# A delta-net inversion with its two 64-blocks overlaid, and 16 row products moved from VectorE to GpSimd and ScalarE

## What is computed

```python
decay = jnp.exp(jnp.where(incl, Gcum[..., :, None] - Gcum[..., None, :], -jnp.inf))
kb = kc * bc[..., None]
A = jnp.where(strict, jnp.einsum('bhnid,bhnjd->bhnij', kb, kc) * decay, 0.0)
t_inv = lax.linalg.triangular_solve(A + eye, jnp.broadcast_to(eye, A.shape), left_side=True, lower=True, unit_diagonal=True)
W = t_inv @ (kb * jnp.exp(Gcum)[..., None])
U = t_inv @ (vc * bc[..., None])
...
v_new = U_n - W_n @ S
o = qd_n @ S + attn_n @ v_new
S = S * gt_n + k_tail_n.T @ v_new
```

## Time and profile before

| | us |
|---|---|
| median of 3 runs | 1768.65 (1767.53 to 1769.34) |
| the profiled execution, its time | 1769.91 |
| its span in the profile | 1768.1 |
| mean granted TensorE clock | 0.992 |
| TensorE busy | 1712.0 (97%) |
| VectorE busy | 1299.4 (73%) |
| ScalarE busy | 1075.2 (61%) |
| GpSimd busy | 161.9 (9%) |

### The profile page before, as it was taken

One profiled execution on the slowest core, in us unless ns is written; L12 is line 12 of the kernel. 1 busy time (PEld: TensorE's weight loads), 2 busy tenths in 40 slices (PEclk: granted clock), 3 DMA queues, 4 the chain that ended last, 5 costly groups with the idle time before them and its releaser, 6 DMA issues.

```text
span 1768.1 us, 34099 instructions
## 1 busy us (share of the span) xinstructions
PE 1712.0 (97%) x11488; PEld 1535.7 (87%) x11488; DVE 1299.4 (73%) x2604; ACT 1075.2 (61%) x2222; POOL 161.9 (9%) x136
## 2 busy tenths in 40 slices
PE   7999998999999999999999999999899999999998
PEld 1877788989999977888899999999799899999997
DVE  3787667767989799667766666666776668878887
ACT  2545466645665699666555555555558666666666
POOL 0000004411638200000000000000010000010000
PEclk9899999999999999999999999999999999999999
DMA  8524441225455411555555555555354544555553
GB/s 301 185 99 143 153 158 62 82 71 190 158 178 188 157 37 38 180 193 196 190 190 184 185 189 185 184 189 190 119 205 143 172 137 134 178 184 185 189 181 129
DMA packets 77271, 283.30 MB, mean 160 GB/s; under 512 B 8576, under 2 KB 8576, under 8 KB 76928
## 3 DMA queue, kind: packets, MB, share of 16 engines
q1 hardware_dynamic: 77184, 282.16, 47.5%
HBM read 281.08 MB, written 1.05 MB: 160 GB/s over the span
## 4 chain that ended last, share of the span: by engine, by line
PE 80%; DVE 11%; ACT 5%; issue 1%; DMA 1%; POOL 1%; PEld 0%; PEldq 0%; SPq 0%; ACTq 0%; POOLq 0%; DVEq 0%
PE banks L901 20%; PE banks L889 17%; PE banks L980 9%; PE banks L491 8%; PE banks L1136 7%; PE banks L1160 3%; PE banks L831 2%; DVE split L2396 2%; DVE arena L2392 2%; PE banks L459 1%; DMA arena<-wstream 1%; PE banks L994 1%; PE banks L680 1%; PE banks L1096 1%; PE banks L665 1%
## 5 line engine op out<-in xcount | busy, mean ns | idle before, releaser
L1501 ACT ACTIVATE split<-arena 128x512 fp32r<-128x512 f32 x492 | 308.9, 629 | 135.0 <-PE banks L889 76.8
L889 PEld LDWEIGHTS banks<-split 128*128 128x128 f32 x2880 | 355.4, 192 | 10.5 <-DVE split L2322 3.1
L901 PE MATMUL banks<-split 128*128 128x512 f32 x1536 | 361.9, 390 | 1.0 <-issue 1.0
L889 PE MATMUL banks<-split 128*128 128x256 f32 x2880 | 358.7, 283 | 3.1 <-DVE split L2322 2.3
L2414 DVE TENSOR_TENSOR split<-arena,split 128x512 fp32r<-128x512 f32 x396 | 270.5, 690 | 105.3 <-ACT split L1501 99.5
L901 PEld LDWEIGHTS banks<-split 128*128 128x128 f32 x1536 | 283.8, 188 | 57.3 <-issue 1.4
L1479 ACT ACTIVATE split<-arena 128x512 fp32r<-128x512 f32 x312 | 194.5, 627 | 115.4 <-PE banks L1136 52.9
L980 PE MATMUL banks<-split 128*128 128x256 f32 x1728 | 218.1, 288 | 4.3 <-DVE split L2492 3.9
L980 PEld LDWEIGHTS banks<-split 128*128 128x128 f32 x1728 | 213.2, 195 | 7.2 <-issue 6.0
L2469 DVE TENSOR_TENSOR split<-arena,split 128x512 fp32r<-128x512 f32 x180 | 123.8, 698 | 67.5 <-ACT split L1479 66.0
L491 PEld LDWEIGHTS banks<-split 128*128 128x128 f32 (+1 forms) x936 | 134.3, 195 | 28.1 <-issue 14.1
(11 more groups left out here) (414 smaller groups left out, 2359.1 us busy)
## 6 DMA issues: line engine op xcount, KB each, us to landing
arena<-wstream SPq DMA_DIRECT2D x525, 512.0 KB, 3.3
arena<-x_t SPq DMA_DIRECT2D x1, 2048.0 KB, 13.0
arena<-matsa SPq DMA_DIRECT2D x1, 1234.0 KB, 6.5
out_t<-arena SPq DMA_DIRECT2D x4, 256.0 KB, 2.0
arena<-mats SPq DMA_DIRECT2D x1, 576.0 KB, 8.3
arena<-crow SPq DMA_DIRECT2D x1, 512.0 KB, 7.3
arena<-rows SPq DMA_DIRECT2D x1, 512.0 KB, 4.0
arena<-mats SPq DMA_DIRECT2D x1, 449.0 KB, 3.7
```

The source lines that it names most:

```text
L889: mm = pe.matmul(ps[:, 4 + b, 0:S], w_parts[:, c, (2 * m + half) % 4, P * k:P * k + P], h_parts[:, e, 4 * half + k, :], start=(half == 0 a ...
L901: mm = pe.matmul(ps[:, 2 * tt + half, :], g_parts[:, e, j % 2, P * tt:P * tt + P], w_parts[:, c, (2 * m + half) % 4, :], start=(first and ...
L1501: act.activation(w_parts[:, 0, (2 * m + half) % 4, :], ring[:, peer_slot(m), 512 * half:512 * half + 512], ACT.Copy).then_inc(sem["w_hi"], 1)
```

## The change

Two things. The first is the layout of the inversion. For l below 6 only the two 64-blocks on the diagonal of each 128x128 matrix hold anything. They are now overlaid: rows 0 to 63 of a tile carry the first block, rows 64 to 127 the second, so a half is 128 elements wide, not 256. The new tile AO holds A in this layout; Z1, Z2 and AO are half as large, and the full inverse is written at l=6 into the new tile Z, whose zero corners are set once.

- `level_products`: product q reads rows 64q to 64q+63 and writes bank 2d+q; so does turn q, with 64 moving columns, into the columns behind the product. For l below 6 turns come first. At l=1 both wait for `w_moved`, the move of W of the step before.
- The mask on VectorE now takes product and turned half together, 2x(128+64) elements, by `masks`, whose last 64 columns are ones; T and ScalarE's move of it are gone. At l=6 VectorE copies the turned halves and the corners.
- `level_update`: each of the two updates writes 64 partitions of bank 2d.
- VectorE's subtraction is 128 elements wide; at l=6 it is a negated copy of 64 partitions by 256.
- `first_inverse` is four instructions of 64 partitions by 128 for a direction, not two of 128 by 256. At l=6 it stands between the copies and the negated copy.
- ScalarE: pack and keep are 128 wide; at l=1 two copies into AO come first, at l=6 keep is two copies of 64 partitions by 256.

The second is the 16 row products. GpSimd multiplies tile by row (`mod_tail`, four for each n, two after scale_tokens and two at the end of its step, all four after scale_tokens for n=3), ScalarE sums the product by a Copy with an accumulated output (`sum_tail`, at the levels listed) and signals `tiles_done`.

The diff, cut to its core:

```diff
         vtok = buf("vtok", 4, 4, P)
         at = buf("at", 4, 4, P)
-        PAIR = ("E", "A0", "A1", "Z0", "Z1", "Z2", "AP", "T", "KB", "VB", "KT", "S", "wt", "uu")
-        pair = [{n: buf(f"{n}{d}", 2 if n == "T" else 4, P) for n in PAIR} for d in range(2)]
-        yp = [buf(f"yp{d}", 2, P) for d in range(2)]
+        PAIR = ("E", "A0", "A1", "Z1", "Z2", "Z", "AO", "AP", "KB", "VB", "KT", "S", "wt", "uu")
+        TWO = ("Z1", "Z2", "AO")
+        pair = [{n: buf(f"{n}{d}", 2 if n in TWO else 3 if n == "AP" else 4, P) for n in PAIR} for d in range(2)]
+        yp = [buf(f"yp{d}", 2, P + 64) for d in range(2)]
+        masks = buf("masks", 5, P + 64)
         assert held["rstd"][0] == held["root"][0] + 512
         osum = arena[:, held["root"][0]:held["root"][0] + 1024].rearrange("p (a b c) -> p a b c", a=2, b=4)
         gbr = [osum[:, d, :, :] for d in range(2)]
...
                 if l == 1:
-                    if n == 0 and d == 1:
+                    if n == 0 and d == 0:
                         pe.wait_ge(sem["proj_free"], 4 + 39)
                     pe.wait_ge(sem["z1_ready"], step_at(n, d))
                 else:
                     pe.wait_ge(sem["z_ready"], level_at(n, l - 1, d))
                     pe.wait_ge(sem["z_kept"], level_at(n, l - 1, d))
                 pe.wait_ge(sem["keys_packed"], level_at(n, l, d))
-                for j in range(2):
-                    c = slice(P * j, P * j + P)
-                    mm = pe.matmul(ps[:, d, c], keys_at(d, l)[:, c], half_at(d, l, 1 - d)[:, c], start=True, stop=True)
-                mm.then_inc(sem["y_done"], 1)
                 if l == 1:
                     if n:
-                        pe.wait_ge(sem["wu_ready"], step_at(n - 1, d))
+                        pe.wait_ge(sem["w_moved"], step_at(n - 1, d))
                     else:
                         pe.wait_ge(sem["tok_ready"], 3 + d)
-                for j in range(2):
-                    mm = pe.transpose(ps[:, 2 + d, P * j:P * j + P], half_at(d, l, d)[:, P * j:P * j + P], ident)
-                mm.then_inc(sem["z_turned"], 1)
+
+                def product(q):
+                    c, r = slice(P * q, P * q + P), rows_at(q if l < 6 else 1 - d)
+                    keys, half = (keys_at(d, l)[r, :], half_at(d, l, 1 - d)[r, :]) if l < 6 else (last_keys(d)[:, c], inverse_at(d, 6)[r, c])
+                    return pe.matmul(level_bank(d, q)[:, 0:P] if l < 6 else level_bank(d, 0)[:, c], keys, half, start=True, stop=True)
+
+                def turn_half(q):
+                    c, r = slice(P * q, P * q + P), rows_at(q if l < 6 else d)
+                    half = half_at(d, l, d)[r, :] if l < 6 else inverse_at(d, 6)[r, c]
+                    return pe.transpose(level_bank(d, q)[:, P:P + 64] if l < 6 else level_bank(d, 1)[:, 64 * q:64 * q + 64], half, ident[r, r])
+
+                if l < 6:
+                    turn_half(0)
+                    turn_half(1).then_inc(sem["y_done"], 1)
+                    product(0)
+                else:
+                    product(0)
+                    turn_half(0)
+                product(1).then_inc(sem["y_done"], 1)
+                if l == 6:
+                    turn_half(1).then_inc(sem["y_done"], 1)
 
             def level_update(n, l, d):
                 pe.wait_ge(sem["y_out"], level_at(n, l, d))
-                pe.wait_ge(sem["t_ready"], level_at(n, l, d))
-                for j in range(2):
-                    mm = pe.matmul(ps[:, d, 256 + P * j:256 + P * j + P], pair[d]["T"][:, j, :], yp[d][:, j, :], start=True, stop=True)
+                for q in range(2):
+                    out = ps[rows_at(q), 2 * d, 256:384] if l < 6 else ps[rows_at(d), 2 * d, 256 + P * q:384 + P * q]
+                    mm = pe.matmul(out, yp[d][:, q, P:P + 64], yp[d][:, q, 0:P], start=True, stop=True)
                 mm.then_inc(sem["p_done"], 1)
 
             def apply_inverse(n, d):
-                b, z = pair[d], pair[d]["Z2"]
+                b, z = pair[d], pair[d]["Z"]
                 pe.wait_ge(sem["z_ready"], level_at(n, 6, d))
                 pe.wait_ge(sem["z_kept"], level_at(n, 6, d))
...
@@ -1376,34 +1396,48 @@
                 rows_of(1, d, dec["G"][:, scan[d][1], 4 * d:4 * d + 4])
 
             def pack_keys(n, l, d):
+                a, over = pair[d][f"A{n % 2}"], pair[d]["AO"].rearrange("p a (b s) -> p (a b) s", s=64)
                 if l == 1:
                     act.wait_ge(*((sem["mask_ready"], d + 1) if n == 0 else (sem["a_beta"], step_at(n - 1, d))))
-                act.activation(as_packed(keys_at(d, l), l), parts(flat(pair[d][f"A{n % 2}"]), l, d), ACT.Copy).then_inc(sem["keys_packed"], 1)
+                    for q in range(2):
+                        o = act.activation(over[rows_at(q)], a[rows_at(q), :, rows_at(q)], ACT.Copy)
+                    link(o)
+                if l < 6:
+                    o = act.activation(as_packed(keys_at(d, l), l), parts(flat(pair[d]["AO"]), l, d), ACT.Copy)
+                else:
+                    o = act.activation(last_keys(d).rearrange("p (g s) -> p g s", s=64), a[rows_at(1 - d), :, rows_at(d)], ACT.Copy)
+                o.then_inc(sem["keys_packed"], 1)
 
             def keep_half(n, l, d):
                 act.wait_ge(*((sem["z1_ready"], step_at(n, d)) if l == 1 else (sem["z_ready"], level_at(n, l - 1, d))))
-                act.activation(next_half(d, l, d), as_next(half_at(d, l, d), l), ACT.Copy).then_inc(sem["z_kept"], 1)
+                if l > 1:
+                    act.wait_ge(sem["z_kept"], level_at(n, l - 1, d))
+                if l < 6:
+                    o = act.activation(next_half(d, l, d), as_next(half_at(d, l, d), l), ACT.Copy)
+                else:
+                    for q in range(2):
+                        r = rows_at(q)
+                        o = act.activation(pair[d]["Z"][r, :, r], inverse_at(d, 6)[r, :].rearrange("p (g s) -> p g s", s=64), ACT.Copy)
+                o.then_inc(sem["z_kept"], 1)
+
+            def sum_tail(a):
+                act.wait_ge(sem["tail_mult"], a - EARLY_TAILS + 1)
+                act.activation(tile_at(tail_at(a)), tile_at(tail_at(a)), ACT.Copy, accum_out=modT[:, 16 + a, 0:1]).then_inc(sem["tiles_done"], 1)
 
             for d in range(2):
                 pack_keys(0, 1, d)
+            tails = iter(range(EARLY_TAILS, 32))
             for n in range(4):
                 for l in range(1, 7):
                     for d in range(2):
                         keep_half(n, l, d)
                     for d in range(2):
-                        if l == 6:
-                            act.wait_ge(sem["y_done"], level_at(n, l, d))
-                            for q in range(2):
-                                r = slice(64 * q, 64 * q + 64)
-                                o = act.activation(yp[d][r, :, r], bank(d, 2, P)[r, :, r], ACT.Copy)
-                            o.then_inc(sem["y_out"], 1)
-                        act.wait_ge(sem["z_turned"], level_at(n, l, d))
-                        act.activation(flat(pair[d]["T"]), ps[:, 2 + d, 0:256], ACT.Copy).then_inc(sem["t_ready"], 1)
-                    for d in range(2):
                         if l < 6:
                             pack_keys(n, l + 1, d)
...
@@ -1420,7 +1454,8 @@
                         act.activation(gain3[:, 0, :], gain3[:, 0, :], ACT.Sqrt)
                 for d in range(2):
                     act.wait_ge(sem["wu_done"], step_at(n, d))
-                    act.activation(pair[d]["wt"].rearrange("p a b -> p (a b)"), ps[:, 2 + d, :], ACT.Copy)
+                    act.activation(pair[d]["wt"].rearrange("p a b -> p (a b)"), ps[:, 2 * d + 1, :], ACT.Copy).then_inc(
+                        sem["w_moved"], 1)
                     act.activation(pair[d]["uu"].rearrange("p a b -> p (a b)"), ps[:, 6 + d, :], ACT.Copy).then_inc(sem["wu_ready"], 1)
             for i, tt in enumerate((1, 0)):
                 if i == 0:
...
@@ -2107,10 +2142,12 @@
 
             def first_inverse(n, d):
                 dve.wait_ge(sem["m_turned"], step_at(n, d))
-                for q in range(2):
-                    o = dve.tensor_tensor(half_at(d, 1, q).rearrange("p (a b s) -> p a b s", a=4, s=2),
-                                          bc(ident.rearrange("p (b q s) -> p b q s", q=2, s=2)[:, :, q, :], 1, 4),
-                                          ps[:, 4 + d, :].rearrange("p (a b q s) -> p a b q s", a=4, q=2, s=2)[:, :, :, q, :], ALU.subtract)
+                for r in (rows_at(0), rows_at(1)):
+                    for q in range(2):
+                        o = dve.tensor_tensor(half_at(d, 1, q)[r, :].rearrange("p (a b s) -> p a b s", a=4, s=2),
+                                              bc(ident[r, r].rearrange("p (b q s) -> p b q s", q=2, s=2)[:, :, q, :], 1, 4),
+                                              bank(4 + d, 4, P)[r, :, r].rearrange("p a (b q s) -> p a b q s", q=2, s=2)[:, :, :, q, :],
+                                              ALU.subtract)
```

(36 more changed lines are left out.)

32 lines of the change are left out of this document (19 added, 13 removed).

## The result

The changed kernel takes 1780.07 us in the median of six runs, the kernel before 1769.09 beside it: ratio 1.0062, 95% interval 1.0047 to 1.0078. It is slower by 0.6%, where 1762.6 us and "faster" were forecast. The profiled execution of the changed kernel took 1781.33 us against 1769.91.

A forecast was written before the change was run, and what follows sets the result against it. TensorE, busy 97% of the span, was taken to bound the kernel, with the inversion a relay between engines. Terms of -10.4 us and +4.3 for the collision gave -6.1: 1763.8 profiled, 1762.6 median, range 1756.5 to 1770.5.

The forecast's parts named there:

- The pieces: Inversion levels: product pair 0.22 us for 0.45, bare level 2.05 for 2.70, level with foreign matrix work 3.5 for 4.34.
- rival C: Inversion levels: halves do not run together, or changing form costs more; 1767 to 1772.8 us; chance 0.22.
- The collision: n=2, l=3: two gap-row tensor_scalars on VectorE each lose one GpSimd product's length on the shared road; +4.3 us.
- rival B: n=2, l=3: no collision, GpSimd's two products fall ahead of the gap rows or past them; 1758.3 us; chance 0.22.
- Part 3, l=6: End of l=6, n=0 to 2: TensorE waits behind VectorE's copies and first_inverse; +1.35, +0.85, +0.2 us.
- Part 4, ScalarE in n=3: n=3: ScalarE gets six sums, 17.5 us of work against 16.9 of TensorE path; +0.6 us.
- rival D: Slower: GpSimd's load with the 16 row products becomes the bound, deciding from 3.8 us a product; 1776 us; chance 0.14.
- Part 3, l=6 of n=3: End of l=6 at n=3: no first_inverse stands there; -0.7 us.
- Part 5, the packing of level 1: Level 1 at the stage's start: two copies go ahead of ScalarE's packing, 0.9 us a direction; +0.3 us for n=0.

The follow-up runs named there:

- mended: Changed kernel with the three moves at once: early28's, the same for products 24 and 25 at n=2, and late_first's; 1764.57 us, ratio 0.9979 to the kernel before.
- late_first: Changed kernel with VectorE's eight first-inverse pieces for the next chunk behind the negated copy that ends l=6, not ahead; 1772.63 us, ratio 1.0017.
- early28: Changed kernel with GpSimd's products 28 and 29 ahead of its scaling of the state for n=3; 1777.42 us, ratio 1.0046.
- warm8: Changed kernel with eight useless matmuls per chunk on TensorE between l=6's last update and the product of inverse and keys; 1778.75 us, ratio 1.0054.
- after_psum: Changed kernel with chunk 3's gap rows kept in PSUM until they are clamped, nothing else; 1778.84 us, ratio 1.0058.
- mended_psum: mended with chunk 3's gap rows kept in PSUM until they are clamped; 1762.25 us, ratio 0.9958.
- overlay_late: Changed kernel with the row products back on VectorE and the first inverse behind the end of l=6; 1766.09 us, ratio 0.9977.
- placed: late_first with all four GpSimd products of n=2 behind the masked queries and ScalarE's sums moved to suit; 1761.11 us, ratio 0.9958.
- mended_warm: mended with the eight useless matmuls per chunk of warm8; 1769.94 us, ratio 1.0009.

## Why the prediction was wrong, by its own steps

Against the profiled executions the forecast was 1763.8 and the time 1781.33, 17.5 us off.

- **The pieces held.** The halves run together: the four matmul instructions of a pair of products take 0.44 us, where one after the other they would take about 0.60 (an estimate, three times 0.11 and 0.27 for the last), and those of the updates, for which no row existed, 0.39 to 0.44. A bare level is 2.05 us, exactly as forecast, a level with foreign work 3.63 (3.5), mask 552 ns, subtraction 288, GpSimd's product 2382 (2350). The prediction's rival C is refuted.
- **The collision held.** -0.8 and +4.3 were forecast for (2,3), and it grew by 3.20 us. VectorE's first clamp and GpSimd's first product came 8.5 us later than forecast, but 0.5 us apart as forecast (328.60 and 329.14 for 320.1 and 320.6). The lock that the Trainium skill describes ("SBUF — State Buffer", section "SBUF: two separate sides") stood beside this reading of the rows, and the clamps of 0.87, 2.45 and 1.87 us agree. It is held for one instruction by the page; the 3.39 us in `mended` go beyond that. The prediction's rival B is refuted.
- **Part 3, l=6: too small.** +1.35, +0.85 and +0.2 were forecast, and it was 2.46, 2.23 and 1.57, 3.9 us more. In the first, from the first product's end to the end of its Z are 4.28 us (281.33 to 285.61), not 3.2: the six copies take 1.61, not 1.2, the eight pieces 2.01, not 1.6, and 0.2 go by before the first copy. A piece takes 283 ns, over the 250 that the prediction named as a sign of its failing. The working had the order right but took it for given; late_first shows that 2.04 us of each tail were the order alone.
- **Part 4, ScalarE in n=3: a wait left out.** +0.6 was forecast from ScalarE's load, and with the level's -0.84 that is -0.24. The step that failed was GpSimd's: no step of the prediction asks when the four products of n=3 can start. They stand behind the scaled state, which waits for the reading of the states for the values (L724, at 356.24) and also for that for the queries, one level later (L733, at 359.87). So product 28 came 3.64 us late for its sum and (3,5) grew by 5.42 us, 5.7 us off; early28 takes 6.1 us out of this level. The prediction's rival D had the right engine and the wrong mechanism: not GpSimd's load (its busy time in the stage is 82.3 us, 84.4 were forecast), but its waits, 33.8 us from its first operation at 260.69 to its last at 376.72, where the prediction left room for 17.
- **The clock: not in the sum at all.** The working took the 1.00 of the earlier trace rows for a property of the stage. The same eight-matmul groups take 1.16 us and 2.08. Levels with the same instructions differ by what a fall costs: (1,1) 10.72 against 8.04 with the gap filled, (3,1) 9.47 against 8.04, (0,2) 4.74 against a forecast 3.69: 5.2 us. A part of (3,5) belongs here as well: where a shorter fall stands behind the same wait, it takes 8.7 us for 9.76.
- **Part 3, l=6 of n=3: a wrong sign.** -0.7 was forecast, because no first inverse stands there. It was +0.4, and +0.2 at full clock (3.25 us in early28 for 3.05 before), 1.1 us off. The copies of l=6, which ScalarE had before, stand on VectorE there too; no run prices them apart.
- **Part 5, the packing of level 1: too small.** +0.3 was forecast for the start. The copies into AO (two for a direction, 0.83 us together) stand ahead of the packing on ScalarE, TensorE waits 1.70 us for it instead of 0.59, and from the first gap rows to Z of (0,1) it took 1.26 us more: 1.0 off. The first fall of the clock begins just behind this wait.
- **What lies before and behind.** The stage began 1.3 us later (253.91 for 252.59). The time at half clock up to there is the same, 13.7 us in both. In the twelve profiled kernels with this opening the stage begins at 251.94 to 253.91, so scatter between executions is enough for it; a share of the changed opening is not ruled out. What follows the stage was 0.9 shorter.

Sum: 3.9 + 5.7 + 5.2 + 1.1 + 1.0 + 1.3 - 0.9 = 17.3 of 17.5 us; the rest is levels of some tenths, in both directions.

Of these the order at l=6, the wait for product 28 and the collision are shown by experiments that take each away in its place, and by the three moves together: 15.7 us were expected from the table of levels and 15.5 came. The price of the clock is read from the trace, and for level 1 shown by warm8 and late_first.

One by one the moves gave 2.7, nothing and 7.4 us in the medians. That a mended wait sends the loss to another level is not shown: the differences to the expected 6.1, 3.5 and 6.1 are smaller than the 4.5 to 9 us by which runs of one of these kernels lie apart, and in the traces of early28 and after_psum the extra falls begin before the edited instructions. The runs of one kernel scatter with its clock: the twelve runs of late_first go from 1768.08 us at a mean clock of 0.992 to 1776.82 at 0.985.

What is not settled is where a fall comes. It follows idle time of TensorE (warm8, late_first, mended_psum), but not each one: the kernel before stands idle for 2.35 us at (1,5), until 308.09, with no fall, and the changed kernel for 1.84 us at (1,6), the same wait that has a fall at (0,6) and (2,6). The fall between 261.8 and 269.7 us, at the stage's start, is in every kernel with the overlay and in none without. No run takes away the copies into AO that stand ahead of it. Whether the row products are better on GpSimd and ScalarE is not settled either. In the mended forms, overlay_late has them on VectorE at 0.9977, placed on the others at 0.9958, intervals that overlap; 5 us between the medians, or 3.4 by the ratios, speak for the move, once its collision is gone.

## What to carry to other kernels

Price a moved operation by its place in each queue, its triggers read from the code one by one, before its duration: here most durations held within some hundredths of a us, and three places cost some 15 us (3 x 2.04, 3.2 and 6.1). When a change takes work from TensorE in a latency-bound stage, take its full clock out of the assumptions. Then runs scatter by several us, and a mended wait is judged by its level in the trace first, and by the median only over many runs. An overlay of halves is worth having (4.34 to 3.63 us a level), and the operation that ends a serial step goes first on its engine, ahead of anything that is only prepared.

## What the runs showed of the hardware that was not expected

- A VectorE operation between SBUF and SBUF is not merely held for the GpSimd instruction in progress. In mended it stayed through three hand-overs of GpSimd, 3.39 us for 0.43, and ended 0.29 us after GpSimd's last operation; beside the products of 2.5 us in the changed kernel it got in at each hand-over. With two SBUF inputs it takes turns instead, and slows GpSimd to 1.50 us for 1.05.
- The same clamp out of PSUM costs 0.69 us instead of 0.43 and was not held up beside GpSimd in either run that has it (mended_psum, after_psum).
- Eight useless matmuls (2.05 us) in an idle time of TensorE kept the clock at 2.4 GHz in level 1 behind it, which was 1.4 to 2.7 us shorter than with a fall. Where the idle time was gone (mended_warm) they cost 1.8 us each time.
